# Two-layer block kernel, state-space stage: heads scanned in pairs on opposite column halves, its outputs and the following projection reordered

## The chip, the cores and the metric

The kernel is one program on one core of a Trainium2 chip. Its time is the device time of one launch in microseconds; the figure shown is the median of the launches timed. Engines are named as the profile names them: PE (matmuls), PEld (PE's weight loads), DVE (VectorE), ACT (ScalarE), POOL (GpSimd), SP (the queue that issues the DMAs).

## What is computed

The whole program is a mixer-and-feed-forward block followed by two more such layers, on 512 tokens of width 1024, in float32. The change touches only the second half of the odd layer's mixer: a Mamba-like state-space scan, a gated norm over its 512 channels, and the projection that takes it and four blocks of a multi-scale pool.

```
dt = softplus(dt_raw + dt_bias);  a = -exp(a_log)
y  = ssd_chunked(xh * dt, dt * a, bm, cm)          # 8 heads of 64, 2 groups, state 128
y  = y + d_skip * xh
y  = rms_norm_2(y * silu(z), ssm_norm)             # over all 512 channels of a token
p  = multiscale_pool(pool_in, pool_w, pool_b, pool_scale)
return concatenate([y, p]) @ w_out                 # 1024 x 1024
```

The kernel does the scan in its quadratic form: for a head, y[t] is the sum over s <= t of (cm[t]·bm[s]) · exp(acs[t] − acs[s]) · x[s], with acs the running sum of dt·a.

## The kernel before

Activations stand with channels on the partitions and the 512 tokens on the free axis, so one tile is 128 x 512; `w` is an array of 50 such tiles, and `ps` is the eight banks of PSUM, each 128 x 512 float32. Weights come as a stream of units of eight 128x128 blocks. SP loads a unit into one of three raw buffers (`Weights.load`, L153), ACT rounds it to the high part (`round_high`, L169), POOL subtracts to get the low part (`subtract_low`, L178), and PE takes a product as three matmuls, high·high, high·low and low·high (L321 to L323). Up to three split units exist at once, and a unit's high part waits until the unit three before it has been released by PE. Each stage writes out by hand the order of every engine's instructions; engines meet only in semaphores that count up, and each engine runs its own list in order.

The steps around the change are, in the list at the end of `network`, `odd_in` (the layer's first projection, which leaves silu(z) in the four tiles from ZG, the convolved x in the four from XS, and the pools' outputs in the four from PO), `x_tok` (`to_token_major`, L709 and L720), `ssd`, `odd_out`, and then the feed-forward.

`stage_ssd` (L3032) walks 32 items: two groups, in each four blocks of 128 source tokens (j), in each four heads. For block j only the tokens from 128·j on matter, so its width is 512, 384, 256 or 128 columns. Once per group and block PE forms the query-key product in float32 (L3048) in bank 0 or 1. For each item PE forms the exponent in bank 2 or 3 by three bf16 matmuls (`decay`, L3053 to L3055), ACT takes its exponential into an SBUF tile (L3080), DVE multiplies that with the query-key bank into another (L3089), and PE multiplies x by it (`values`, L3062). That last matmul has 64 columns of weights, and its output goes to the lower or the upper 64 partitions of bank 4 + head//2, by the head's parity. The list of PE is decay(0), then decay(n+1), values(n) for each n, so that two values matmuls always have the three matmuls of a decay between them. A float32 matmul of the program is two matmul instructions in the trace. After the last item DVE adds the skip term (L3095) and applies the gate (L3097), tile by tile.

`odd_out` is `stage_linear` with `before=ssm_norm()`. The norm's part on PE, `factor_pe`, comes first: `column_sums` (L444) over the four tiles of squares, which ACT takes from the gated outputs (L653), then, after a square root on ACT (L464) and a reciprocal on DVE (L470), `spread_columns` (L450). Then `first_products` (L329) makes the first three output tiles at once, input block by input block, in the order 4, 5, 6, 7 (the pools) and 0, 1, 2, 3 (the scan): for each of the first six blocks the high parts of the three (L341, L342) and then the low parts (L347), and the last two blocks output tile by output tile. The high and low parts of all eight blocks are made in this stage by ACT (L649) and DVE (L666), in `odd_split`, tiles 0 to 15; DVE scales the four scan tiles by the factor in bank 7 (L674). ACT begins the stage with the third weight unit that these products need (L2041), POOL with its low part. After the three tiles there is a mean (L2012) and the rest of the product (L321 to L323).

Two other places in the kernel put half-column matmuls next to each other and serve as measures: `narrow_halves` (L391), eight matmuls of 128x64 weights on 512 columns, alternating between the lower and the upper half of bank 4, and the values of the band attention (L1020), for its first pair one matmul of 128 columns on each half.

Of the kernel before, what the change touches and what calls it, by code (L numbers as in the profile page):

```python
# [20 lines left out]
P = 128  # L21
T = 512
# [161 lines left out]
class Before:  # L184
# [3 lines left out]
    def __init__(self, pe, act, dve, pool, high, ready, counts, order=tuple(range(KD))):  # L188
        self.order = order
        self.pe, self.act, self.dve, self.pool, self.counts = pe, act, dve, pool, counts  # L190
        self.high, self.ready = high, ready
# [9 lines left out]
def network(nc, x_t, vectors, constants, rel_rev, stream, bias_line, bias_rows, gate_rows, out_t):  # L201
    n_units = stream.shape[0]
    ctx = ExitStack()
    with ctx:
# [26 lines left out]
        odd_split = split_over("odd_split", 0, KD)  # L231
# [97 lines left out]
        def first_products(pe, rhs, before):  # L329
# [307 lines left out]

        def ssm_norm():

            SQS = 28  # L640
            dst = odd_split

            def pe(p):
                p.wait_ge(norm_act.sem, norm_act.at(4))
                factor_pe(p, [w[:, SQS + t, :] for t in range(4)])

            def act(a):
                def high(t):
                    S.activation(dst[:, 0, t, :], w[:, YS + t, :], ACT.Copy).then_inc(norm_high.sem, 1)  # L649
# [12 lines left out]

            def dve(d):
                def low(t, n):
                    d.wait_ge(norm_high.sem, norm_high.at(n))
                    V.tensor_tensor(dst[:, 1, t, :], w[:, YS + t, :], dst[:, 0, t, :].bitcast(F32),  # L666
                                    ALU.subtract).then_inc(norm_low.sem, 1)

                low(4, 1)
                low(5, 2)  # L670
                factor_dve(d, 5)
                d.wait_ge(norm_pe.sem, norm_pe.at(2))
                for t in range(4):
                    V.scalar_tensor_tensor(w[:, YS + t, :], w[:, YS + t, :], v("ssm_norm", t), bank(FACTOR), ALU.mult,  # L674
                                           ALU.mult).then_inc(norm_dve.sem, 1)
                low(6, 3)
                low(7, 4)
                for t in range(4):
                    low(t, t + 5)

            def place(t):
                return t + 5 if t < 4 else t - 3

            def high_ready(p, t):
                p.wait_ge(norm_high.sem, norm_high.at(place(t)))

            def ready(p, t):
                p.wait_ge(norm_low.sem, norm_low.at(place(t)))

            return Before(pe=pe, act=act, dve=dve, pool=nothing, high=high_ready, ready=ready,  # L690
                          order=(4, 5, 6, 7, 0, 1, 2, 3),
                          counts=((norm_pe, 2), (norm_act, 5), (norm_dve, 5), (norm_high, KD), (norm_low, KD),
                                  (dve_out2, 4)))
# [2195 lines left out]
        XTK, YS, PO = 16, 20, 24  # L2889
# [142 lines left out]
        def stage_ssd():  # L3032


            items = [(g, j, hh) for g in range(2) for j in range(NT) for hh in range(4)]
            n_items = len(items)
            e = [w[:, 46, :], w[:, 47, :]]
            m_ = [w[:, 48, :], w[:, 49, :]]
            @block.tensor
            def _(pe):  # L3040
                def decay(n):
                    g, j, hh = items[n]
                    a, wd = j * P, T - j * P
                    hd = 4 * g + hh
                    if hh == 0:
                        if n >= 8:
                            pe.wait_ge(dve_out.sem, dve_out.at(n - 4))
                        TE.matmul(bank((n // 4) % 2, 0, wd), w[:, BM + g, a:a + P], w[:, CMM + g, a:T],  # L3048
                                  start=True, stop=True)
                    if n >= 2:  # L3050
                        pe.wait_ge(act_out.sem, act_out.at(n - 1))
                    d = bank(2 + n % 2, 0, wd)
                    TE.matmul(d, one_hot(hd, P), row_parts(SSD_PARTS, 0)[:, a:T], start=True, stop=False)  # L3053
                    TE.matmul(d, row_parts(SSD_PARTS, 1)[:, a:a + P], one_hot(hd, wd), start=False, stop=False)
                    TE.matmul(bank(2 + n % 2, 0, P), ident_h[:, :], diag_st_h[:, :], start=False,  # L3055
                              stop=True).then_inc(tile_ready.sem, 1)

                def values(n):
                    g, j, hh = items[n]
                    hd = 4 * g + hh  # L3060
                    pe.wait_ge(dve_out.sem, dve_out.at(n + 1))
                    TE.matmul(bank(4 + hd // 2, j * P, T - j * P, half(hd)), w[:, XTK + j, hd * HD:(hd + 1) * HD],  # L3062
                              m_[n % 2][:, 0:T - j * P], start=(j == 0), stop=(j == NT - 1)
                              ).then_inc(pe_out.sem, 1)
# [3 lines left out]
                for n in range(n_items):  # L3068
                    if n + 1 < n_items:
                        decay(n + 1)  # L3070
                    values(n)

            @block.scalar
            def _(act):
                for n, (g, j, hh) in enumerate(items):
                    wd = T - j * P
                    act.wait_ge(tile_ready.sem, tile_ready.at(n + 1))
                    if n >= 2:
                        act.wait_ge(dve_out.sem, dve_out.at(n - 1))
                    S.activation(e[n % 2][:, 0:wd], bank(2 + n % 2, 0, wd), ACT.Exp).then_inc(act_out.sem, 1)  # L3080

            @block.vector
            def _(dve):
                for n, (g, j, hh) in enumerate(items):
                    wd = T - j * P
                    dve.wait_ge(act_out.sem, act_out.at(n + 1))
                    if n >= 2:
                        dve.wait_ge(pe_out.sem, pe_out.at(n - 1))
                    V.tensor_tensor(m_[n % 2][:, 0:wd], bank((n // 4) % 2, 0, wd), e[n % 2][:, 0:wd],  # L3089
                                    ALU.mult).then_inc(dve_out.sem, 1)  # L3090

                dve.wait_ge(pe_out.sem, pe_out.at(n_items))
                for t in range(4):
                    y = w[:, YS + t, :]
                    dve_chain.link(dve, V.scalar_tensor_tensor(y, w[:, XS + t, :], v("d_skip", t), bank(4 + t),  # L3095
                                                               ALU.mult, ALU.add))
                    V.tensor_tensor(y, y, w[:, ZG + t, :], ALU.mult).then_inc(dve_out2.sem, 1)  # L3097
            tile_ready.close(n_items)
            pe_out.close(n_items)
            act_out.close(n_items)  # L3100
            dve_out.close(n_items)

        def stage_last():
# [44 lines left out]
            ("odd_out", lambda: stage_linear(KD, of(odd_split), "residual", sums="both",  # L3148
# [142 lines left out]
```

## Time and profile before

| | us |
|---|---|
| median of 3 runs (2282.13 to 2284.49) | 2283.25 |
| the profiled execution's own time | 2289.55 |
| its span, first to last instruction | 2287.8 |
| PE busy | 2175.1 (95%) |
| PE weight loads busy | 1754.6 (77%) |
| DVE busy | 996.6 (44%) |
| ACT busy | 839.3 (37%) |
| POOL busy | 818.8 (36%) |

Mean granted TensorE clock of the core: 0.960 of full speed. The chain of work that ended last runs through PE for 86% of the span, through DVE for 8%, ACT for 2% and DMA for 1%. A busy figure is the time in which at least one instruction of an engine was under way; matmuls are pipelined, so PE's is not PE at its peak, and the chain, which counts from one start to the next, is the better measure of what a matmul costs.

### The profile page before, as it was taken

To read this page: it belongs to the slowest core of one execution; us is meant where nothing else is said; L and a number is where in the kernel's file an instruction comes from. 1 tells how busy PE (TensorE), PEld (TensorE's weight loads), DVE (VectorE), ACT (ScalarE), POOL (GpSimd) and SP (SyncE) were. 2 spreads that over 40 slices of the span, in tenths; PEclk is the share of its full clock that TensorE was granted. 3 is DMA by queue.
4 is the path that set the end of the run, shared out by engine and by line. 5 is a ranking of instruction groups with operands and counts; after the bars stand their busy time and mean duration, and the time that the engine had idled before them with its cause. 6 is when DMAs were issued, how large, how long until landed. Compare 5 with 4: busy or idle time off the path is not lost.

```text
span 2287.8 us, 29687 instructions
## 1 busy us (share of the span) xinstructions
PE 2175.1 (95%) x12396; PEld 1754.6 (77%) x12404; DVE 996.6 (44%) x1622; ACT 839.3 (37%) x1284; POOL 818.8 (36%) x362
## 2 busy tenths in 40 slices
PE   7999989999899999999998899999999889999997
PEld 6767778888778888777776678888877477888886
DVE  4222855435631022345337644442268465444323
ACT  4345521133342243243334344442243334444322
POOL 4423300034334444453231344444444035444442
PEclk9999978799999999999999899999999989999998
DMA  7222200014223233222111123323212012332331
GB/s 260 92 74 84 74 2 3 2 56 149 73 83 101 92 102 101 92 65 74 56 56 37 47 92 97 105 93 101 92 64 83 19 56 68 104 96 92 102 100 57
DMA packets 53006, 182.98 MB, mean 80 GB/s; under 512 B 5752, under 2 KB 5760, under 8 KB 52744
## 3 DMA queue, kind: packets, MB, share of 16 engines
q1 hardware_dynamic: 52872, 181.08, 24.6%
q8 instruction: 98, 1.61, 0.3%
q14 instruction: 36, 0.29, 0.0%
HBM read 176.32 MB, written 7.62 MB: 80 GB/s over the span
## 4 chain that ended last, share of the span: by engine, by line
PE 86%; DVE 8%; ACT 2%; DMA 1%; issue 1%; POOL 1%; SPq 0%; DVEq 0%; ACTq 0%
PE ps L321 20%; PE ps L323 20%; PE ps L322 20%; PE ps L1519 3%; PE ps L2526 2%; PE ps L2528 1%; PE ps L2527 1%; PE ps L341 1%; PE ps L347 1%; PE ps L342 1%; PE ps L1049 1%; DMA raw_units<-stream 1%; PE ps L3062 1%; PE ps L1051 1%; PE ps L1050 1%
## 5 line engine op out<-in xcount | busy, mean ns | idle before, releaser
L178 POOL TENSOR_TENSOR split_units<-raw_units,split_units 128x1024 fp32r<-128x1024 f32 x314 | 760.3, 2430 | 1414.5 <-ACT split_units L169 1414.5
L321 PE MATMUL ps<-x_split,split_units 128*128 128x512 f32 x1224 | 483.3, 395 | 10.1 <-POOL split_units L178 7.8
L322 PE MATMUL ps<-x_split,split_units 128*128 128x512 f32 x1224 | 478.7, 391 | 0.0
L323 PE MATMUL ps<-x_split,split_units 128*128 128x512 f32 x1224 | 478.2, 391 | 0.0
L169 ACT ACTIVATE split_units<-raw_units 128x1024 fp32r<-128x1024 f32 x314 | 330.0, 1052 | 387.3 <-PE ps L323 337.9
L321 PEld LDWEIGHTS ps<-x_split,split_units 128*128 128x128 f32 x1224 | 231.1, 189 | 64.5 <-issue 8.0
L322 PEld LDWEIGHTS ps<-x_split,split_units 128*128 128x128 f32 x1224 | 231.1, 189 | 49.4 <-issue 1.7
L323 PEld LDWEIGHTS ps<-x_split,split_units 128*128 128x128 f32 x1224 | 231.2, 189 | 48.7
L321 PE MATMUL ps<-hidden_split,split_units 128*128 128x512 f32 x608 | 237.3, 390 | 0.0
L323 PE MATMUL ps<-hidden_split,split_units 128*128 128x512 f32 x608 | 236.6, 389 | 0.0
L322 PE MATMUL ps<-hidden_split,split_units 128*128 128x512 f32 x608 | 236.5, 389 | 0.0
L2857 DVE SCALAR_TENSOR_TENSOR work<-ps,vec,work 128x511 f32<-128x511 f32 x88 | 66.0, 750 | 225.3 <-ACT work L2846 225.0
L321 PEld LDWEIGHTS ps<-hidden_split,split_units 128*128 128x128 f32 x608 | 114.1, 188 | 24.2 <-issue 0.5
L322 PEld LDWEIGHTS ps<-hidden_split,split_units 128*128 128x128 f32 x608 | 114.1, 188 | 24.1 <-issue 0.5
L323 PEld LDWEIGHTS ps<-hidden_split,split_units 128*128 128x128 f32 x608 | 114.1, 188 | 23.7
L2846 ACT ACTIVATE work<-ps,vec 128x512 f32<-128x512 f32 x88 | 68.7, 781 | 167.9 <-PE ps L323 150.2
L2086 DVE TENSOR_TENSOR x<-x,ps 128x512 f32<-128x512 f32 x29 | 19.9, 688 | 142.4 <-PE ps L323 141.9
L2859 DVE SCALAR_TENSOR_TENSOR work<-ps,vec,work 128x510 f32<-128x510 f32 x88 | 65.9, 749 | 3.1
L2837 ACT ACTIVATE hidden_split<-work 128x512 fp32r<-128x512 f32 x44 | 27.8, 632 | 103.2 <-DVE work L2867 103.2
L1519 PE MATMUL ps<-work 64*64 64x64 f32 x1920 | 62.8, 229 | 0.0
L1519 PEld LDWEIGHTS ps<-work 64*64 64x64 f32 x1920 | 62.5, 146 | 0.0
L341 PE MATMUL ps<-x_split,split_units 128*128 128x512 f32 x120 | 50.8, 423 | 10.6 <-ACT x_split L599 5.0
(436 smaller groups left out, 3274.1 us busy)
## 6 DMA issues: line engine op xcount, KB each, us to landing
raw_units<-stream SPq DMA_DIRECT2D x314, 512.0 KB, 3.5
bias_rows<-bias_line SPq DMA_DIRECT2D x1, 2816.0 KB
gate_rows<-work SPq DMA_DIRECT2D x10, 256.0 KB, 2.1
work<-gate_rows SPq DMA_DIRECT2D x10, 256.0 KB, 2.7
x<-x_t SPq DMA_DIRECT2D x4, 512.0 KB, 6.6
work<-bias_rows SPq DMA_DIRECT2D x1, 2048.0 KB
out_t<-x SPq DMA_DIRECT2D x8, 256.0 KB
vec<-vectors SPq DMA_DIRECT2D x1, 1159.5 KB, 8.6
```

The lines of the kernel that those rows point to most:

```text
L169: scalar.activation(self.split[:, u % SPLIT, 0, :], self.raw[:, u % RING, :], ACT.Copy).then_inc(self.high_done, 1)
L178: gpsimd.tensor_tensor(self.split[:, u % SPLIT, 1, :], self.raw[:, u % RING, :], self.split[:, u % SPLIT, 0, :].bitcast(F32), ALU.subtract ...
L321: TE.matmul(out, high, rhs(0, k), start=(k == 0), stop=False)
L322: TE.matmul(out, high, rhs(1, k), start=False, stop=False)
L323: ins = TE.matmul(out, low, rhs(0, k), start=False, stop=last and shift is None)
L341: TE.matmul(bank(m), high, rhs(0, k), start=(i == 0), stop=False)
L1519: ins = TE.matmul(ps[r, out, i * HD:(i + 1) * HD], left(i, r), right(i, r), start=True, stop=True)
L2526: TE.matmul(bank(b % 2), high, a[0], start=(k == 0), stop=False)
L2837: S.activation(hidden2[:, 0, j, :], w[:, y0 + 2 * j % 4, :], ACT.Copy).then_inc(high_out.sem, 1)
L2846: S.activation(w[:, y0 + m % 4, :], bank(m % 4), ACT.Identity, scale=taps(m)[2], bias=v("ffn_b", layer * 44 + (m % 2) * FF2 + m // 2)).the ...
L2857: dve_chain.link(dve, V.scalar_tensor_tensor(y[:, 1:T], b[:, 0:T - 1], taps(m)[1], y[:, 1:T], ALU.mult, ALU.add))
L2859: V.scalar_tensor_tensor(y[:, 2:T], b[:, 0:T - 2], taps(m)[0], y[:, 2:T], ALU.mult, ALU.add).then_inc(tile_read.sem, 1)
```

## The change

The items become 16 pairs of heads. PE runs two pairs of decays ahead instead of one head, in banks 2 and 3 and, for the odd pairs, 6 and 7; the two values matmuls of a pair stand next to each other, one on each column half. ACT writes its exponentials into tiles 46 to 49 and DVE multiplies in place, so the exponential of pair p waits for the values of pair p − 2. Group 1 reuses banks 4 and 5, so its first values wait for DVE's skip terms of tiles 0 and 1, which now stand behind pair 8; the gates of these two tiles stand behind pairs 9 and 10, their squares (ACT) behind pairs 11 and 12, the sum of these squares (DVE) behind pair 14. The high parts of the pools' blocks are taken by ACT behind pairs 1 to 4, the low parts by POOL. In `odd_out` nothing stands on PE ahead of the products; the column sums come after two input blocks, the spreading after three. The sums are over two tiles instead of four.

```diff
             for i in range(UNIT - APART):
+                if i in before.among:
+                    before.among[i](pe)
                 before.high(pe, before.order[i])
...
-        odd_split = split_over("odd_split", 0, KD)
+        ssm_split, pool_split = split_over("ssm_split", 0, 4), split_over("pool_split", 32, 4)
...
         def ssm_norm():
-            def pe(p):
-                p.wait_ge(norm_act.sem, norm_act.at(4))
-                factor_pe(p, [w[:, SQS + t, :] for t in range(4)])
+            def sums(p):
+                p.wait_ge(norm_dve.sem, norm_dve.at(1))
+                p.wait_ge(norm_act.sem, norm_act.at(4))
+                column_sums(p, SUMS, 4, (w[:, SQS, :], w[:, SQS + 3, :]))
+            def spread(p):
+                p.wait_ge(norm_dve.sem, norm_dve.at(2))
+                spread_columns(p, FACTOR, 8)
             def act(a):
-                for t in range(4):
+                for t in (2, 3):
                     a.wait_ge(dve_out2.sem, dve_out2.at(t + 1))
                     S.activation(w[:, SQS + t, :], w[:, YS + t, :], ACT.Square).then_inc(norm_act.sem, 1)
-                high(4)
-                high(5)
                 factor_act(a, 1, LN_EPS, mean_of=HALF)
-                high(6)
-                high(7)
                 for t in range(4):
-                    a.wait_ge(norm_dve.sem, norm_dve.at(t + 2))
-                    high(t)
+                    a.wait_ge(norm_dve.sem, norm_dve.at(t + 3))
+                    S.activation(ssm_split[:, 0, t, :], w[:, YS + t, :], ACT.Copy).then_inc(norm_high.sem, 1)
             def dve(d):
+                d.wait_ge(norm_act.sem, norm_act.at(3))
+                V.tensor_tensor(w[:, SQS, :], w[:, SQS, :], w[:, SQS + 2, :], ALU.add).then_inc(norm_dve.sem, 1)
                 factor_dve(d, 5)
                 d.wait_ge(norm_pe.sem, norm_pe.at(2))
+                for t in range(5):
+                    if t < 4:
+                        V.scalar_tensor_tensor(w[:, YS + t, :], ...).then_inc(norm_dve.sem, 1)
+                    if t >= 1:
+                        low(t - 1)
+            return Before(pe=nothing, ..., order=(4, 5, 6, 7, 0, 1, 2, 3), among={2: sums, 3: spread}, ...)
...
         def stage_ssd():
-            items = [(g, j, hh) for g in range(2) for j in range(NT) for hh in range(4)]
+            items = [(g, j, pr) for g in range(2) for j in range(NT) for pr in range(2)]
+            FIRST = n_items // 2
+            POOL_AT, GATE_AT, SQUARE_AT, ADD_AT = 1, FIRST + 1, FIRST + 3, FIRST + 6
...
+                def values(p):
+                    g, j, pr = items[p]
+                    pe.wait_ge(dve_out.sem, dve_out.at(2 * p + 2))
+                    if g == 1 and j == 0:
+                        pe.wait_ge(side_dve.sem, side_dve.at(pr + 1))
+                    for hh in range(2):
+                        hd = 4 * g + 2 * pr + hh
+                        ins = TE.matmul(bank(4 + pr, j * P, T - j * P, half(hh)),
+                                        w[:, XTK + j, hd * HD:(hd + 1) * HD], weights(p, hh)[:, 0:T - j * P],
+                                        start=(j == 0), stop=(j == NT - 1))
+                    ins.then_inc(pe_out.sem, 1)
                 decay(0)
-                for n in range(n_items):
-                    if n + 1 < n_items:
-                        decay(n + 1)
-                    values(n)
+                decay(1)
+                for p in range(n_items):
+                    if p + 2 < n_items:
+                        decay(p + 2)
+                    values(p)
+            @block.gpsimd
+            def _(pool):
+                for t in range(4):
+                    pool.wait_ge(norm_high.sem, norm_high.at(t + 1))
+                    G.tensor_tensor(pool_split[:, 1, t, :], w[:, PO + t, :], pool_split[:, 0, t, :].bitcast(F32),
+                                    ALU.subtract).then_inc(norm_low2.sem, 1)
             @block.scalar
+                for p, (g, j, pr) in enumerate(items):
+                    for hh in range(2):
+                        act.wait_ge(tile_ready.sem, tile_ready.at(2 * p + hh + 1))
+                        if p >= 2:
+                            act.wait_ge(pe_out.sem, pe_out.at(p - 1))
+                        S.activation(weights(p, hh)[:, 0:wd], bank(decay_bank(p, hh), 0, wd), ACT.Exp)
+                    t = p - POOL_AT
+                    if 0 <= t < 4:
+                        S.activation(pool_split[:, 0, t, :], w[:, PO + t, :], ACT.Copy).then_inc(norm_high.sem, 1)
+                    t = p - SQUARE_AT
+                    if 0 <= t < 2:
+                        act.wait_ge(dve_out2.sem, dve_out2.at(t + 1))
+                        S.activation(w[:, SQS + t, :], w[:, YS + t, :], ACT.Square).then_inc(norm_act.sem, 1)
             @block.vector
+                    for hh in range(2):
+                        dve.wait_ge(act_out.sem, act_out.at(2 * p + hh + 1))
+                        a = weights(p, hh)[:, 0:wd]
+                        V.tensor_tensor(a, bank((p // 2) % 2, 0, wd), a, ALU.mult).then_inc(dve_out.sem, 1)
+                    if p == FIRST:
+                        dve.wait_ge(pe_out.sem, pe_out.at(FIRST))
+                        skipped(0)
+                        skipped(1)
+                    if 0 <= p - GATE_AT < 2:
+                        gated(p - GATE_AT)
+                    if p == ADD_AT:
+                        dve.wait_ge(norm_act.sem, norm_act.at(2))
+                        dve_chain.link(dve, V.tensor_tensor(w[:, SQS, :], w[:, SQS, :], w[:, SQS + 1, :], ALU.add))
                 dve.wait_ge(pe_out.sem, pe_out.at(n_items))
-                for t in range(4):
-                    dve_chain.link(dve, V.scalar_tensor_tensor(y, ..., bank(4 + t), ALU.mult, ALU.add))
-                    V.tensor_tensor(y, y, w[:, ZG + t, :], ALU.mult).then_inc(dve_out2.sem, 1)
+                skipped(2)
+                skipped(3)
+                gated(2)
+                gated(3)
```

## Rows read from the trace of the kernel before

**Rows 1.** Busy time, granted clock (PEclk) and DMA of stretches of the span.
```profile
core 0: us, PE busy (x) PEld busy (x) DVE busy (x) ACT busy (x) POOL busy (x), PEclk, DMA share, GB/s
1786.80:1829.80 43.00, 41.05 (x174) 15.46 (x176) 15.63 (x32) 14.67 (x33) 0.00 (x0) 1.00 0.00 1
1829.80:1865.10 35.30, 26.77 (x113) 23.43 (x113) 15.71 (x23) 10.94 (x17) 3.63 (x2) 0.76 0.05 15
...
1847.00:1850.60 3.60, 3.60 (x11) 2.87 (x11) 3.14 (x5) 2.29 (x4) 0.00 (x0) 0.51 0.00 0
```
**Rows 2.** Chain that ended last, one head at each width: start, us, what.
```profile
1791.51 1.00 PE ps L3062 x2
...
1796.82 0.79 PE ps L3062 x2
...
1805.25 0.06 PE ps L3054
...
1805.36 0.58 PE ps L3062 x2
...
1807.61 0.36 PE ps L3062 x2
```
**Rows 3.** Timeline of PE: half-column matmuls as neighbours, one alone, and what follows.
```profile
1692.03 3.65 PE L391 MATMUL ps<-x,vec 128*64 128x512 f32 x16
1695.61 0.50 PE L321 MATMUL ps<-x_split,split_units 128*128 128x512 f32 x1
...
1791.29 0.22 PE L3055 MATMUL ps<-diag_st_h,ident_h 128*128 128x128 bf16 x1
1791.44 1.07 PE L3062 MATMUL ps<-work 128*64 128x512 f32 x2
...
98.26 0.44 PE L1020 MATMUL ps<-work 128*64 128x128 f32 x4
98.63 0.50 PE L1049 MATMUL ps<-x_split,split_units 128*128 128x512 f32 x1
```
**Rows 4.** Groups of the scan on ACT and DVE by form, 512 columns wide.
```profile
L3089 DVE TENSOR_TENSOR work<-ps,work 128x512 f32<-128x512 f32 x8 | 5.4, 690 | 9.6 <-ACT work L3080 9.6
L3080 ACT ACTIVATE work<-ps 128x512 f32<-128x512 f32 x8 | 4.7, 596 | 11.6 <-PE ps L3055 11.6
```
**Rows 5.** Timeline around the end of the scan: weight unit, skip term, gate.
```profile
1828.90 1.05 ACT L169 ACTIVATE split_units<-raw_units 128x1024 fp32r<-128x1024 f32 x1
...
1829.86 0.75 DVE L3095 SCALAR_TENSOR_TENSOR work<-work,vec,ps 128x512 f32<-128x512 f32 x1 [0.53 <-PE ps L3062]
1830.03 2.34 POOL L178 TENSOR_TENSOR split_units<-raw_units,split_units 128x1024 fp32r<-128x1024 f32 x1 [49.98 <-ACT split_units L169]
1830.64 2.28 DVE L3097 TENSOR_TENSOR work<-work 128x512 f32<-128x512 f32 x1
```
**Rows 6.** Chain that ended last, from the last gate to the products.
```profile
1836.38 0.70 DVE work L3097
1837.10 0.64 ACT work L653
1837.79 7.00 PE ps L444 x32
...
1845.34 2.08 PE ps L450 x8
1847.42 0.43 PE ps L341
...
1851.44 0.23 PE ps L341
```
**Rows 7.** Timeline: the norm's sums and spreading elsewhere, at full clock and after.
```profile
33.50 1.05 PE L450 MATMUL ps<-con,col 128*128 128x128 f32 x8
...
1895.36 1.95 PE L444 MATMUL ps<-ones,work 128*128 128x1 f32 x16 [0.79 <-DVE work L2095]
...
1899.23 2.08 PE L450 MATMUL ps<-con,col 128*128 128x128 f32 x8 [0.93 <-DVE col L470]
```

More of the change, by code:

```diff
@@ L184, with __init__ @@
 class Before:
-    def __init__(self, pe, act, dve, pool, high, ready, counts, order=tuple(range(KD))):
-        self.order = order
+    def __init__(self, pe, act, dve, pool, high, ready, counts, order=tuple(range(KD)), among=None):
+        self.order, self.among = order, among or {}
         self.pe, self.act, self.dve, self.pool, self.counts = pe, act, dve, pool, counts
@@ L676, in dve @@
[L676 to L682, printed above, removed]
+                for t in range(5):
+                    if t < 4:
+                        V.scalar_tensor_tensor(w[:, YS + t, :], w[:, YS + t, :], v("ssm_norm", t), bank(FACTOR),
+                                               ALU.mult, ALU.mult).then_inc(norm_dve.sem, 1)
+                    if t >= 1:
+                        low(t - 1)
@@ L684, in high_ready @@
             def high_ready(p, t):
-                p.wait_ge(norm_high.sem, norm_high.at(place(t)))
+                p.wait_ge(norm_high.sem, norm_high.at(t + 5 if t < 4 else t - 3))
             def ready(p, t):
[L688 to L693, printed above, removed]
+                if t < 4:
+                    p.wait_ge(norm_low.sem, norm_low.at(t + 1))
+                else:
+                    p.wait_ge(norm_low2.sem, norm_low2.at(t - 3))
@@ L696, in to_token_major @@
+            return Before(pe=nothing, act=act, dve=dve, pool=nothing, high=high_ready, ready=ready,
+                          order=(4, 5, 6, 7, 0, 1, 2, 3), among={2: sums, 3: spread},
+                          counts=((norm_pe, 2), (norm_act, 5), (norm_dve, 6), (norm_high, KD), (norm_low, 4),
+                                  (norm_low2, 4), (dve_out2, 4)))
         def to_token_major(jobs, read, scaled=None):
@@ L3032, in stage_ssd, with weights @@
         def stage_ssd():
[L3035 removed]
+            items = [(g, j, pr) for g in range(2) for j in range(NT) for pr in range(2)]
             n_items = len(items)
[L3037 to L3038 removed]
+            FIRST = n_items // 2
+            POOL_AT, GATE_AT, SQUARE_AT, ADD_AT = 1, FIRST + 1, FIRST + 3, FIRST + 6
+            def weights(p, hh):
+                return w[:, 46 + 2 * (p % 2) + hh, :]
@@ L3039, in _, with decay_bank, decay @@
+            def decay_bank(p, hh):
+                return 2 + 4 * (p % 2) + hh
             @block.tensor
             def _(pe):
-                def decay(n):
-                    g, j, hh = items[n]
+                def decay(p):
+                    g, j, pr = items[p]
                     a, wd = j * P, T - j * P
[L3044 to L3048, printed above, removed]
-                                  start=True, stop=True)
[L3050 to L3064, printed above, removed]
+                    if pr == 0:
+                        if p >= 4:
+                            pe.wait_ge(dve_out.sem, dve_out.at(2 * (p - 2)))
+                        TE.matmul(bank((p // 2) % 2, 0, wd), w[:, BM + g, a:a + P], w[:, CMM + g, a:T],
+                                  start=True, stop=True)
@@ L3093, in _, with skipped @@
[L3093 to L3096, printed above, removed]
-                    V.tensor_tensor(y, y, w[:, ZG + t, :], ALU.mult).then_inc(dve_out2.sem, 1)
-            tile_ready.close(n_items)
+                def skipped(t):
+                    V.scalar_tensor_tensor(w[:, YS + t, :], w[:, XS + t, :], v("d_skip", t), bank(4 + t % 2),
+                                           ALU.mult, ALU.add).then_inc(side_dve.sem, 1)
@@ L3147, in network @@
             ("ssd", stage_ssd),
-            ("odd_out", lambda: stage_linear(KD, of(odd_split), "residual", sums="both",
+            ("odd_out", lambda: stage_linear(KD, odd_half, "residual", sums="both",
                                              before=ssm_norm())),
```

53 lines of the change are left out of this document (28 added, 25 removed).

## The prediction

> **What bounds the kernel now.** I read the table of stretches first, cut where the change begins and ends: from the first query-key matmul of the scan (1786.8) to its last values matmul (1829.8), and from there to the end of the first three output tiles of `odd_out` (1865.1). These are 43.0 and 35.3 us, 78.3 in all, and nothing outside them is touched. In the first stretch the granted clock is 1.00 (2.4 GHz), DVE and ACT are busy for 15.6 and 14.7 us, POOL and the DMAs not at all, and PE for 41.05 of 43.0 us: the scan is bound by PE, and PE idles 1.95 us in it. In the second one the mean clock is 0.76 [rows 1].
>
> Then the chain of waits, to see what PE's time goes to. The values matmul of one head takes 1.00 us of the chain at width 512, 0.79 at 384, 0.58 at 256 and 0.36 at 128 [rows 2]. Each has 64 columns of weights, so it uses half of the array. Eight heads at each width make 8 × 2.73 = 21.8 us, half of the scan. ACT takes 0.60 and DVE 0.69 us for one head at 512 columns [rows 4], less than PE's 1.6 (1.00 and a decay of some 0.6). So two engines have slack and PE has none.
>
> After the scan the chain leaves PE for 8.0 us (1829.8 to 1837.8): DVE's four skip terms and gates, and ACT's last square. The first gate takes 2.28 us, against 0.70 for the last, while POOL's subtraction of a weight unit runs (1830.03 to 1832.37) [rows 5, 6]. PE comes back at half clock: 7.00 us for 32 matmuls of the sums, 0.55 for root and reciprocal, 2.08 for the spreading, and its first products come at 0.43 us each instead of 0.23 [rows 6], 1.2 GHz up to 1850.6 [rows 1]. The products themselves need no sum before their fifth input block.
>
> **The scan, part by part.** *Values in pairs.* What does a pair on opposite halves cost? Where the trace has such neighbours, the two matmuls of 128 columns took 0.37 us to the next start, where one alone takes 0.36; and eight of 512 columns took 3.58 us, 0.45 each, where one alone takes 1.00 [rows 2, 3]. So the second half is nearly free. The bounds are a free second half (0) and none of it free (a full single). I take 0.05 us more than a single: 1.05, 0.84, 0.63, 0.41, four pairs of each, 11.7 us. Saved: 21.8 − 11.7 = 10.1 us.
>
> *Changes between full and half columns.* The third decay matmul starts 0.15 us before a values matmul, though 128 columns of it take 0.06 [rows 2, 3]: 0.09 us for each entry, and 16 fewer of them save 1.4 us. The query-key and decay matmuls stay as they are.
>
> *Waits.* With two pairs of decays ahead, let me see whether ACT and DVE keep up. The exponentials of pair p wait for the values of p − 2. At width 512 two of them and the multiplication behind the second take 2 × 0.60 + 0.69 and some 0.15 of signals, 2.05 us [rows 4]. Meanwhile PE has two decays (1.1), a pair of values (1.05) and two decays again (1.1) to do, 3.25 us. The slack of 1.2 us shrinks with the width to about 0.25 at 128. ACT's four copies for the pools (0.64 each, as a square [rows 6]) stand where the exponentials have to wait for values anyway; only the last, at width 256, delays, by about 0.25 us, and that is inside the slack. POOL's four subtractions of 512 columns, half of 2.34 us each [rows 5], have an idle queue and 43 us. Behind pair 8 DVE waits for the last values of group 0 and adds two skip terms (2 × 0.75): the multiplications of pair 9 are queued behind these, but PE has the query-key matmul of the next block and two decays first; this costs nothing to 0.3 us. The values of pairs 8 and 9 wait for these skip terms, which end sooner than the multiplications. The sum of squares behind pair 14 (0.7) has no cover: the last multiplications are queued behind it and there is no decay left, so it costs its 0.4 to 0.7 us. In all I leave PE 1.25 us of idle time for the 1.95 of before: 0.7 us saved.
>
> The scan: 10.1 + 1.4 + 0.7 = 12.2 us; 43.0 becomes 30.8.
>
> **From the end of the scan.** *Products first.* 72 matmuls at 0.2275 us (the chain's 0.23 at full clock [rows 6]) are 16.4 us. PE can start at once on the first two output tiles, but the third needs the third weight unit. ACT rounds that behind its last exponential and POOL subtracts behind ACT; before, it ended 3.47 us after ACT began [rows 5]. ACT's last exponential will end about 1.1 us ahead of the last values, so the unit is there 2.4 us after the end. PE has 0.9 us of work until then and idles 1.5. This is the late one now, and the norm is not: gate 2 waits for POOL and ends at 3.0 us, gate 3 at 3.7, the last square at 4.3, while PE comes to the sums only at 2.4 + 3.2 = 5.6 us.
>
> *The norm.* 16 matmuls of sums instead of 32, at full clock: 1.95 us, as elsewhere; the spreading 1.05 [rows 7]. Root and reciprocal (0.55) pass beside the third block of products (2.05). Scaling a tile (0.75), its copy (0.64) and its subtraction (0.7) stand beside 2.05 us of products per block and one whole block lies between; if that cover were gone, 2.1 us would show once. ACT's and DVE's work for the pools' blocks is out of this stage.
>
> So 16.4 + 1.5 + 1.95 + 1.05 = 20.9 us for 35.3: 14.4 saved.
>
> **Sum.** 12.2 + 14.4 = 26.6 us. The profiled execution's own 2289.55 becomes 2263.0; it stands 6.3 above the median, of which none is seen in these stretches, so the median 2283.25 becomes 2256.7. What a measurement can tell from no change is about 0.2%, 4.6 us.
>
> **Rivals.** *The pair overlaps only in part (8%).* A float32 matmul is two instructions; if the second head's first had to wait for the first head's second, three streams would follow one another where two suffice: 0.43, 0.32, 0.21 and 0.11 us more per pair, 4.3 in all, and 2261.0. Against it stands the isolated pair of 0.37 us [rows 3]; for it, that no isolated pair of 512 half columns is there. The Trainium skill speaks for this one (TensorE: Matmul & The Clock Gate, Packing small matmuls): matmuls start and end strictly in program order. The isolated pair of 128 columns does not bear it out: by it, that pair would take some 0.46 us, and it took 0.37.
>
> *It does not overlap (5%).* Then the values save nothing, at most 10.1 us back: 2266.8. Against it: eight in 3.58 us.
>
> *The clock falls in the norm (12%).* Sums of one column are light work; at 1895.36 they ran at full rate, but the spreading that followed a little later took 2.08 us instead of 1.05 [rows 7]. In the changed kernel a stretch of PE idling 1.5 us, then sums, stands among the products. If the clock falls there, the spreading costs 1.0 more, the sums up to 1.9, and up to 3.6 us of products at the low level (as from 1847.0 to 1850.6 [rows 1]) 1.8 more: 2258.5 to 2261.5. Against it: dense products stand on both sides.
>
> *Slower (3%).* The clock would have to be down through the scan: it is the only mechanism of the right size. PE's 29.7 us of scan work would double to 59.4, and 3.6 us of products run cold after it (1.8): 2256.7 + 29.7 + 1.8 = 2288.2, slower by 4.9 us. It decides only if nearly all of the scan runs at 1.2 GHz; with half of it the kernel is still faster. Against it: clock 1.00 in the whole of the scan of before, with half of the array idle half of the time and PE waiting more.
>
> *It doesn't do what it says (2%):* another unit or wait, unseen here, holds PE back until the norm is done, and the second stretch stays near its old length: 2271.
>
> **The numbers.** The forecast has 70%, with a range of its own from 2253 (no idle in the scan, a pair at no more than a single, a stall of 0.5) to 2259.5 (waits of 2 us more and a run's scatter of 1). The first three rivals reach 2261.5 and, at the end, 2266.8. The range of 8 in 10 is 2252.5 to 2263.5; it leaves out those that do not overlap and the slower ones. All cases but the slower one are faster by over 4.6 us: with part of its 3% and something for what I have not seen given to no change, that is 0.96 faster, 0.02 within, 0.02 slower.
>
> **What would show it.** In the scan: 31 us between the first L3048-like matmul and the last values, four values instructions of 512 columns in some 1.05 us of the chain, PE idle for 1 to 1.5 us with the largest wait before the last values. After it: no gap of 8 us, the clock at 1.00 through to the third tile, a wait of 1.5 us for POOL's unit, sums of 16 in 1.95 us, spreading in 1.05 us, the products' third tile 21 us after the scan's end. Wrong would be: a pair at 1.5 us or 1.9 (no full overlap), a clock of 0.5 anywhere in it, DVE rather than PE at the end of the waits of pairs 8 to 11, or a wait before the sums.

## The result, and the profile after

The changed kernel took 2258.95 us, the median of 5 runs (2252.35 to 2262.54), against 2284.49 (2282.13 to 2289.44) for the kernel before on the same chip. The ratio on record is 0.9874, with a 95% interval of 0.9855 to 0.9893: faster by 28.8 us, between 24.4 and 33.1. It is not the quotient of these two medians, which lie 25.5 us apart (0.9888). The forecast was 26.6 us less and 2256.7 us. The profiled execution took 2258.95 us (span 2257.2), 30.6 less than the one of before.

First the table of stretches of the changed kernel, with the columns of [rows 1] and cut at the same places: from the first query-key matmul to the end of the last values matmul, and from there to the end of the third output tile. A third one lies further on.

```profile
1786.58:1815.90 29.32, 28.25 (x175) 12.94 (x177) 16.97 (x37) 17.45 (x40) 5.08 (x4) 1.00 0.00 1
1815.90:1836.70 20.80, 19.42 (x97) 16.16 (x97) 10.56 (x16) 7.43 (x11) 3.67 (x2) 1.00 0.09 26
...
1866.70:1916.70 50.00, 46.19 (x203) 38.48 (x204) 24.88 (x41) 25.63 (x37) 26.67 (x15) 0.93 0.20 64
```

The scan went from 43.0 to 29.3 us, the second stretch from 35.3 to 20.8, with the clock at 1.00 where it was 0.76. That is 13.7 + 14.5 = 28.2 us. The other 2.4 us of the 30.6 lie outside of the change, 0.2 ahead of it and 2.2 behind: the norm of the feed-forward, some 30 us later, ran at a mean clock of 0.93 here and at 0.90 in the corresponding 50 us of the kernel before, in code that both have in common.

The chain of waits of the changed kernel, in the scan and from its end on (start, us, what):

```profile
1788.27 1.28 ACT L3104
...
1804.13 0.84 PE ps L3056 x2
...
1805.74 1.01 PE ps L3075 x4
1806.75 0.27 PE ps L3063
...
1807.23 0.16 PE ps L3063
...
1809.80 0.80 PE ps L3075 x4
...
1813.83 0.61 PE ps L3075 x4
1814.69 0.27 ACT work L3104
1814.96 0.95 ACT split_units L169
1815.98 2.38 POOL split_units L178
1818.41 0.50 PE ps L341
...
1821.89 1.68 PE ps L446 x16
...
1825.78 0.89 PE ps L452 x8
```

A pair of values matmuls (L3075, four instructions) now takes 1.01 us at width 512 and 0.80 at 384, where one head alone took 1.00 and 0.79 [rows 2]: the second head costs 0.01. The 8 us on DVE, ACT and an idle PE behind the scan [rows 5, 6] are gone; what the chain names there is the third weight unit, ACT's rounding and POOL's subtraction, for which PE waits. The sums take 1.7 us for 16 instead of 7.0 for 32, the spreading 0.9 instead of 2.1.

The timeline around the end of the scan shows what is late now, and what is not:

```profile
1814.20 0.68 DVE L3139 TENSOR_TENSOR work<-work 128x512 f32<-128x512 f32 x1
1814.52 0.45 ACT L3104 ACTIVATE work<-ps 128x128 f32<-128x128 f32 x2 [0.58 <-PE ps L3075]
1814.85 1.06 ACT L169 ACTIVATE split_units<-raw_units 128x1024 fp32r<-128x1024 f32 x1
1815.47 0.44 PE L3075 MATMUL ps<-work 128*64 128x128 f32 x4 [0.68 <-DVE work L3130]
1815.98 2.37 POOL L178 TENSOR_TENSOR split_units<-raw_units,split_units 128x1024 fp32r<-128x1024 f32 x1 [16.88 <-ACT split_units L169]
1817.28 2.23 DVE L3122 TENSOR_TENSOR work<-work 128x512 f32<-128x512 f32 x2
1818.41 0.50 PE L341 MATMUL ps<-pool_split,split_units 128*128 128x512 f32 x1 [1.38 <-POOL split_units L178]
1818.94 1.23 ACT L659 ACTIVATE work<-work 128x512 f32<-128x512 f32 x2 [3.03 <-DVE work L3122]
1821.73 1.84 PE L446 MATMUL ps<-ones,work 128*128 128x1 f32 x16
```

The two gates (L3122) take 2.23 us, as the first one runs beside POOL's subtraction (with that moved away they take 1.29, further on); the last square ends at 1820.17, 4.3 us after the scan, and PE comes to the sums at 5.8. PE waits 0.68 us before the last pair of values, and 1.38 us for the third unit.

### The profile page after: what moved, and what is told of

The parts are those of the page before. It is cut to its first block, busy times and chain, and to the rows that moved or that the text cites. A ratio compares the mean times of both kernels' runs of the same rounds, so it can differ in the third digit from the quotient of the medians.

```text
span 2257.2 us, 29630 instructions
## 1 busy us (share of the span) xinstructions
PE 2153.4 (95%) x12380; PEld 1743.6 (77%) x12388; DVE 992.0 (44%) x1620; ACT 837.1 (37%) x1284; POOL 823.6 (36%) x366
## 4 chain that ended last, share of the span: by engine, by line
PE 86%; DVE 8%; ACT 2%; DMA 1%; issue 1%; POOL 1%; SPq 0%; DVEq 0%; ACTq 0%
PE ps L321 20%; PE ps L323 20%; PE ps L322 20%; PE ps L1520 3%; PE ps L2527 2%; PE ps L2529 1%; PE ps L2528 1%; PE ps L347 1%; PE ps L341 1%; PE ps L342 1%; PE ps L1050 1%; DMA raw_units<-stream 1%; POOL split_units L178 1%; PE ps L1052 1%; PE ps L1051 1%
```

## The experiments

Whole times scatter by 3 to 12 us over the runs of one kernel on one chip (12 runs of the kernel before: 2281.67 to 2293.23). In the profiled executions the scan's start alone lies anywhere from 1779.3 to 1786.8, in code that all of them share. The two stretches, on the other hand, agree to 0.1 us between two executions of the changed kernel. So the experiments are read from the stretches, and whole times are given beside them. Line numbers of a varied kernel can differ by a few from those of the changed one.

### Both heads of a pair on the same half

```diff
-                        hd = 4 * g + 2 * pr + hh
+                        hd = 4 * g + pr + 2 * hh
-                        ins = TE.matmul(bank(4 + pr, j * P, T - j * P, half(hh)),
+                        ins = TE.matmul(bank(4 + hh, j * P, T - j * P, half(pr)),
```

> The changed kernel with the heads paired as (0, 2) and (1, 3) of a group instead of (0, 1) and (2, 3): the two values matmuls still stand next to each other, but both on the same column half, in two banks. The result is the same computation. Scan = first query-key matmul to the end of the last values matmul (43.0 us before the change, 29.3 after). Theory (the pair is cheap because its two halves of the array run together): a pair then costs about 0.85, 0.64, 0.43 and 0.21 us more at the four widths, four pairs each, 8.5 us more in all, scan about 38 us. Rival (the gain is that two values matmuls stand together, with fewer changes between full and half columns and fewer waits; halves don't matter): scan 29.3 to 30 us. Pair 8 also waits for both skip terms here, at most 0.5 us.

The median was 2263.51 us (ratio to the kernel before 0.9881, 0.986 to 0.9902). The stretches, and the chain in the scan at width 512:

```profile
1779.30:1817.20 37.90, 36.41 (x175) 16.98 (x178) 17.14 (x38) 17.46 (x40) 5.20 (x5) 1.00 0.00 1
1817.20:1837.80 20.60, 19.41 (x97) 16.16 (x98) 10.38 (x16) 7.44 (x10) 3.59 (x2) 1.00 0.10 27
```
```profile
1787.10 1.86 PE ps L3075 x4
```

The scan takes 37.9 us, 8.6 more than in the changed kernel, and a pair 1.86 us instead of 1.01; the surcharge is 0.85, 0.63, 0.43 and 0.22 us at the four widths, one more stream of that width each time. So the two halves of the array do run together, in float32 with different moving data on each. Besides the half, the bank differs: the two heads of a pair now write two banks, where in the changed kernel they share one. No run has opposite halves in two banks, or one half in one bank; that the half decides and not the bank is argued from the size of the surcharge. The rival without overlap is dead as a description of the change, and the one with half an overlap too: it asked for 1.48 us.

### A decay between the two heads

```diff
-                    if p + 2 < n_items:
-                        decay(p + 2)
-                    values(p)
+                    for hh in range(2):
+                        if p + 2 < n_items:
+                            decay(p + 2, (hh,))
+                        values(p, (hh,))
```

> The changed kernel with a decay of one head between the two values matmuls of a pair (decay head 0, values head 0, decay head 1, values head 1), for all pairs but the last two, which have no decays left. Theory: full-column matmuls between them end the overlap, so every values matmul costs its single price again (1.00, 0.79, 0.58, 0.36), and there are 14 more entries at 0.09 us: about 10 + 1.3 us more, scan 40 to 41 us. Rival (order does not matter as the halves are free of each other anyway, or the gain came from looking two pairs ahead): scan about 30 us.

The median was 2272.39 us (0.9927, 0.991 to 0.9944).

```profile
1785.20:1826.40 41.20, 39.53 (x175) 15.22 (x177) 17.16 (x37) 17.42 (x40) 5.05 (x4) 1.00 0.00 1
...
1826.40:1828.90 2.50, 1.13 (x6) 0.61 (x4) 2.44 (x3) 0.04 (x1) 2.37 (x1) 0.89 0.00 0
1828.90:1832.00 3.10, 3.07 (x8) 2.44 (x9) 1.97 (x4) 2.52 (x3) 0.00 (x0) 0.54 0.58 172
```

The scan takes 41.2 us, at the upper end of what was expected, and the chain has the single price again for each head:

```profile
1791.67 1.00 PE ps L3075 x2
```

With full-column matmuls between them, opposite halves give nothing. From the two runs the scan's 13.7 us come apart, roughly. From 43.0 to 41.2 (1.8) more than one thing changes: the last two pairs of this run have no decay left to stand between their heads, so they still overlap (some 0.9 us), PE idles 0.3 us less, and the rest is not told apart; what looking two pairs ahead is worth by itself no run shows. From 41.2 to 37.9 (3.3) it is standing next to each other: two heads on one half take 1.86 us where two apart take 2.00, and one change to full columns falls away for each pair. From 37.9 to 29.3 (8.6) it is the opposite halves.

The second stretch came out at 22.1 us instead of 20.8, which was not asked for. Behind PE's wait of 1.40 us for the third unit the clock is at 0.54 for the next 3.1 us. The changed kernel has the same wait, 1.38 us, and kept its clock in both of its profiled executions.

### The norm first, all else as changed

```diff
+            def first(p):
+                sums(p)
+                spread(p)
-            return Before(pe=nothing, ..., among={2: sums, 3: spread},
+            return Before(pe=first, ...,
```

> The changed kernel with the column sums and the spreading ahead of all products of odd_out, as before the change; all else as changed (sums over two tiles, gates and squares of the first two tiles beside the scan, pools' blocks ready). Second stretch = end of the scan to the end of the third output tile (35.3 us before the change, 20.8 after). Theory A (the order is what saves, and the clock follows PE's idle time): PE idles about 4.4 us until the sum of squares is there, the clock falls to half, sums 3.5 us, 0.55, spreading 2.1, then products 16.4 us with some 1.3 us for their first part at half clock: 28 us. Theory B (a gap of 4.4 us leaves the clock at full): 4.4 + 1.95 + 0.55 + 1.05 + 16.4 = 24.4 us.

The median was 2267.52 us (0.9903, 0.9886 to 0.992). The chain has 3.59 us for the sums and 2.08 for the spreading, and these stretches, the last of them the whole second one:

```profile
1814.70:1819.20 4.50, 0.01 (x2) 0.00 (x0) 4.36 (x6) 1.47 (x4) 2.35 (x1) 0.91 0.22 44
1819.20:1822.80 3.60, 3.57 (x16) 3.49 (x16) 0.00 (x0) 1.05 (x1) 0.00 (x0) 0.50 0.24 93
1822.80:1829.00 6.20, 5.65 (x18) 4.85 (x19) 3.68 (x7) 2.16 (x4) 0.00 (x0) 0.53 0.00 0
...
1814.70:1843.20 28.50, 23.44 (x99) 20.04 (x98) 10.53 (x16) 7.44 (x11) 3.69 (x2) 0.82 0.07 19
```

Theory A: 28.5 us from the scan's end to the third tile. PE idles 4.5 us and then runs at 1.2 GHz for nearly 10 us. Products first save 7.7 us here; 3.1 us of these are the longer idle time (4.5 for 1.4), 0.6 the wait for root and reciprocal, which nothing covers now, and the remaining 4 us are in the main the clock (1.9 in the sums, 1.2 in the spreading).

### The products first, in the kernel before

The scan is left as it was; ACT copies the pools' blocks behind heads 1 to 4, POOL subtracts beside the scan, and `odd_out` has the products first with sums over four tiles.

```diff
+                    t = n - 1
+                    if 0 <= t < 4:
+                        S.activation(pool_split[:, 0, t, :], w[:, PO + t, :], ACT.Copy).then_inc(norm_high.sem, 1)
...
-            return Before(pe=pe, ..., pool=nothing, high=high_ready, ready=ready,
+            return Before(pe=nothing, ..., among={2: sums, 3: spread},
```

> The kernel before with the second part of the change alone: the scan head by head as it was, the pools' high parts on ACT behind heads 1 to 4 and their low parts on POOL during the scan, products first in odd_out, sums (over four tiles, 32 matmuls) after two input blocks, spreading after three. Theory: the scan stays at 43.0 us; in the second stretch PE waits 1.6 us for the third weight unit, reaches the sums 5.7 us after the scan, waits 2.3 us more for gates and squares, sums 3.9 us, spreading 1.05, products 16.4: 25.3 us against 35.3, 10 us faster than before in all. Rival (moving the products changes the second stretch only together with the gates beside the scan): PE waits at the sums much longer and the stretch stays above 30 us. If the clock falls in the wait at the sums, 28 to 29 us.

The median was 2277.49 us (0.9959, 0.9941 to 0.9976), and the scan 43.0 us: the copies and POOL's work cost it nothing. The last row is the whole second stretch.

```profile
1825.10:1829.50 4.40, 2.90 (x12) 2.07 (x13) 4.32 (x5) 0.74 (x2) 2.36 (x1) 1.00 0.20 28
1829.50:1833.00 3.50, 1.68 (x8) 1.05 (x6) 2.92 (x6) 1.88 (x3) 0.00 (x0) 1.00 0.28 115
1833.00:1837.80 4.80, 4.74 (x33) 4.74 (x33) 0.00 (x0) 1.29 (x2) 0.00 (x0) 0.77 0.00 0
1837.80:1842.00 4.20, 4.20 (x12) 3.33 (x12) 0.18 (x1) 0.26 (x1) 0.00 (x0) 0.50 0.02 4
...
1825.10:1853.10 28.00, 24.62 (x112) 20.55 (x113) 13.41 (x19) 8.83 (x13) 3.67 (x2) 0.88 0.07 19
```

The second stretch takes 28.0 us, not the 25.3 of the theory but the branch of the expectation in which the clock falls: PE idles 1.5 us for the unit, 1.9 for the last square, and the clock goes down within the sums. So the order of the products without the shorter norm leaves 28.0 us, and the shorter norm with the first two gates and squares beside the scan, without the order (above), 28.5: 7.3 and 6.8 us for 14.5 together. Both have the pools' blocks ready beside the scan, whose own share no run tells.

### Gates and squares of the first two tiles behind the scan

```diff
-                    if 0 <= p - GATE_AT < 2:
-                        gated(p - GATE_AT)
...
+                gated(0)
+                gated(1)
                 gated(2)
```

> The changed kernel with the gates and squares of the first two tiles back behind the scan; their skip terms stay beside it, since group 1 reuses their banks. Products first, sums over two tiles, as changed. Scan 29.3 us and second stretch 20.8 us in the changed kernel. Theory A (the gates beside the scan are worth little, since PE reaches the sums only 5.6 us after the scan): the last square ends about 5.8 us after the scan's end, the sum of squares 6.5, so PE waits up to 1 us at the sums: second stretch 21 to 22 us, scan 29.2. Theory B (a second wait of PE soon after the one for the third unit takes the clock down, as it did where the products alone were moved): sums, spreading and one to two blocks at half clock, 24 to 26 us.

Their addition moves along with the squares.

```profile
1780.20:1809.40 29.20, 28.23 (x175) 12.91 (x177) 15.34 (x34) 16.35 (x38) 5.07 (x4) 1.00 0.00 1
1809.40:1831.00 21.60, 19.64 (x96) 16.07 (x97) 12.56 (x19) 8.73 (x13) 3.67 (x2) 1.00 0.08 25
```
```profile
1815.94 1.95 PE L446 MATMUL ps<-ones,work 128*128 128x1 f32 x16 [0.48 <-DVE work L674]
```

Theory A: scan 29.2, second stretch 21.6. Gates and squares beside the scan are worth 0.8 us in the second stretch once the products stand first, and cost the scan 0.1. This kernel ran once (2255.45 us). PE waits 1.48 us for the unit and, 3.5 us later, 0.48 at the sums; the clock did not fall.

### The third weight unit during the scan

```diff
                 for p, (g, j, pr) in enumerate(items):
...
+                    if p == 5:
+                        wts.high_part(act, S)
...
-                    wts.round_high(act, S, u0 + 1)
                     before.act(act)
...
+                wts.low_part(pool, G)
```

> The changed kernel with the third weight unit rounded by ACT behind pair 5 and subtracted by POOL behind the pools' blocks, both during the scan, instead of at the start of odd_out. Theory: PE's wait of 1.4 us, 0.9 us into the products, is gone, and the gates of tiles 2 and 3 no longer stand behind POOL (2.2 us for two, should be 1.4): second stretch 19.4 us instead of 20.8, clock 1.00 throughout; scan unchanged at 29.3, or 0.3 us longer where ACT's 1.05 us stands at width 256. Rival (something else is as late as the unit: a buffer or the gates): 20.3 us or more, with a wait at the sums.

The median was 2252.06 us (0.9845, 0.9821 to 0.9869).

```profile
1779.40:1808.70 29.30, 28.21 (x175) 12.90 (x177) 16.95 (x37) 17.36 (x40) 7.43 (x5) 1.00 0.06 19
1808.70:1827.90 19.20, 19.20 (x99) 16.30 (x98) 9.62 (x16) 7.43 (x10) 1.35 (x1) 1.00 0.01 1
```
```profile
1810.11 1.29 DVE L3132 TENSOR_TENSOR work<-work 128x512 f32<-128x512 f32 x2
```

The second stretch takes 19.2 us, with PE busy all the time: it is now nothing but matmuls. The two gates take 1.29 us instead of 2.23, with POOL idle beside them. The scan is as long as in the changed kernel. Its median lies 5.3 us below the changed kernel's on the same chip (2257.34, further on); of these only 1.6 are shown to be the edit's.

### The same, and the exponential's table loaded early

```diff
-                act.wait_ge(tile_read.sem, tile_read.at(0))
                 for p, (g, j, pr) in enumerate(items):
...
+                    if t == 0:
+                        act.wait_ge(tile_read.sem, tile_read.at(0))
```

> As the kernel with the early third unit, and ACT's wait for the stage before moved from ahead of the first exponential to ahead of the first copy. In the changed kernel the table for the exponential was loaded (1.28 us) only when the first exponent was there; before the change it was loaded 5 us earlier. Theory: the load stands ahead of the wait again, the first exponential starts 1.3 us earlier, of which PE gains only the 0.3 us by which it waited for the first pair, since it has two pairs of decays to do: scan 29.0, second stretch 19.4, 1.7 us less than the changed kernel over both. Rival: the scan gains the whole 1.3 us.

```profile
1785.70:1814.60 28.90, 28.09 (x175) 13.11 (x178) 16.97 (x37) 16.09 (x39) 7.44 (x5) 1.00 0.06 19
1814.60:1833.70 19.10, 19.10 (x96) 16.19 (x97) 9.62 (x16) 7.43 (x10) 1.31 (x1) 1.00 0.00 1
```

The scan took 28.9 us and the second stretch 19.1, near the theory's 29.0 and 19.4: of the load's 1.28 us PE feels 0.4. The median was 2258.87 us (0.9873, 0.9851 to 0.9895), 1.5 us above that of the changed kernel on the same chip; the 2.1 us won in the stretches cannot be seen in it.

### The changed kernel again

> The changed kernel once more, unchanged, beside the others: scan 29.3 us, second stretch 20.8 us if the clock stays up behind PE's wait of 1.4 us for the third unit, or 22.1 us if it falls there for the 2.5 us that it fell in the kernel with the values apart. Whole times should again scatter by some 10 us from run to run, by what lies outside of these two stretches.

29.3 and 20.8 us, clock 1.00; the median was 2257.34 us (0.9865, 0.9843 to 0.9887; 2250.94 to 2259.47).

### The sum of squares behind the scan, and a ring of four pairs

Both start from the kernel with unit and table early. The first moves the addition of pair 14 into the norm. The second is

```diff
-                return w[:, 46 + 2 * (p % 2) + hh, :]
+                return w[:, (46, 48, 12, 14)[p % 4] + hh, :]
-                        if p >= 2:
-                            act.wait_ge(pe_out.sem, pe_out.at(p - 1))
+                        if p >= 4:
+                            act.wait_ge(pe_out.sem, pe_out.at(p - 3))
```

> The kernel with the early third unit and the early table (scan 28.8 us, second stretch 19.15), with the sum of the first two squares moved from behind pair 14 to behind the scan. The prediction priced it at 0.4 to 0.7 us of the scan, as the last multiplications are queued behind it. Theory A (the prediction's): scan 28.1 to 28.4. Theory B (what holds the last pair is the exponential, which waits for the values of pair 13, and the sum stands almost wholly beside that): scan 28.7. The sums of the norm start when PE reaches them, 4.1 us after the scan's end, or up to 0.3 us later, as one more sum stands ahead of them on DVE.

> The kernel with the early third unit and the early table, and the exponentials written to a ring of four pairs (tiles 46 to 49 and 12 to 15, which the pools no longer need) instead of two: the exponential of pair p waits for the values of p - 4 instead of p - 2. Theory: the waits of PE before the last pairs (0.7 us before pair 15) shrink, as the exponentials can run ahead as far as the two pairs of decay banks let them; scan 28.1 to 28.4 us instead of 28.8, second stretch 19.15. Rival (PE's own work bounds the scan but for the start, and the last wait is the sum of squares on DVE): scan 28.7 to 28.8.

```profile
1785.80:1814.50 28.70, 28.11 (x177) 13.03 (x177) 16.37 (x36) 16.08 (x39) 7.45 (x5) 1.00 0.06 19
1814.50:1833.90 19.40, 19.40 (x98) 16.19 (x97) 10.31 (x17) 7.43 (x10) 1.31 (x1) 1.00 0.00 1
```
```profile
1785.80:1813.80 28.00, 27.96 (x177) 13.12 (x177) 17.01 (x37) 16.16 (x39) 7.45 (x5) 1.00 0.07 20
1813.80:1833.00 19.20, 19.20 (x99) 16.30 (x98) 9.62 (x16) 7.43 (x10) 1.36 (x1) 1.00 0.00 1
```

Moving the addition (first fence) wins 0.1 to 0.2 us in the scan and loses 0.2 to 0.3 behind it; this kernel ran once (2258.43 us). The ring of four (second fence) wins 0.8 to 0.9 in the scan: PE is busy for 27.96 of 28.0 us. Its two stretches are 47.2 us, against 50.1 in the changed kernel and 78.3 before. Its median was 2259.33 us (0.987, 0.9851 to 0.9889), which cannot be told from the changed kernel's: in the part that the change touches it is 2.9 us better, and the scatter of the whole is larger than that.

## Why the prediction was right, and where its terms were off

The time forecast was 2256.7, measured 2258.95, inside of the range; the gain forecast was 26.6 us and the interval is 24.4 to 33.1. By the stretches it was 28.2: the scan gave 1.5 us more than forecast and the second stretch 0.1 more. With a scatter of some 10 us between single executions, that the whole time came within 2.3 us of the forecast is in part luck; the stretches are the test.

*What bounds the scan.* PE, as read. That PE keeps the pace in pairs too, is shown by the busy times: 28.25 of 29.32 us.

*Values in pairs:* 11.7 us forecast, 4 × (1.01 + 0.80 + 0.58 + 0.37) = 11.0 measured. The lower bound, a free second half, was nearly right; that it comes from the halves is what the pair on one half speaks for.

*Changes between full and half columns.* 1.4 us forecast, at 0.09 for each entry to half columns. The chain shows the price on the way back: the first decay matmul takes 0.27 us at width 384 behind values, 0.16 behind another decay, 0.11 less once for each pair, which makes an estimated 1.8.

*Waits.* 1.25 us of idle PE forecast, 1.07 measured, with the largest wait before the last values, as forecast, but not for the reason given. The sum of squares, priced at 0.4 to 0.7, is worth 0.1 to 0.2: the step "there is no decay left, so it costs" overlooked that the exponential of pair 15 is held by the values of pair 13 (the 0.58 us wait for L3075 at 1814.52), and the addition (1814.20 to 1814.88) stands beside that. The ring of four shows it: the wait is gone, for 0.8 us. And the table load was not in the forecast: it came back onto the path with a wait put ahead of the first exponential, at 0.4 us. The 0.28 us that PE waited before the first pair and the 0.68 before the last make up nearly all of its idle time. 12.2 us were forecast for the scan and 13.7 came; values (0.7), changes (0.4) and idle time (0.2) account for 1.3 of the 1.5 missing, and the other 0.2 stay open.

*Behind the scan:* 20.9 forecast, 20.8 measured, with small errors that cancel. The wait for the third unit was 1.4 for 1.5, the last square 4.3 us after the scan for 4.3, the sums reached at 5.8 for 5.6, and the sums and the spreading took 1.7 and 0.9 us of the chain for 1.95 and 1.05. The forecast had added their whole durations (1.84 in the timeline here), where the chain counts from start to start; the products took by difference 16.9 us for 16.4. That the unit is the late thing is shown by its being moved: 1.6 us, with the gates no longer beside POOL.

*The rivals.* Half an overlap and none: fell with 1.01 us for a pair of 512 columns. The rule of the Trainium skill behind the first (TensorE: Matmul & The Clock Gate, Packing small matmuls), that matmuls start and end in program order, did not bring what the rival read from it: four instructions in 1.01 us leave no room for three streams in a row, which would take 1.48. In what order the four ended, the merged rows do not show. The fall of the clock did not come in the two executions of the changed kernel that were profiled, but it came in its variants: behind the wait for the unit with the values apart (1.3 us), behind the 4.5 us of idle time with the norm first, and with the products alone moved, where a wait of 1.5 us was followed by one of 1.9. It did not come with the gates last, where the second wait was 0.5 us. So the price was of the right kind, but it falls behind waits of PE, not with the one-column sums as such: these ran at full clock in the changed kernel. The slower case had no sign of itself: 1.00 through every scan. (Its sum has 29.7 us for PE's work in the scan; 41.05 − 10.1 − 1.4 is 29.55, which changes nothing.)

What stays open is why the clock held behind a wait of 1.2 to 1.5 us for the unit in three kernels and fell in one, and what makes the whole time scatter ahead of the scan.

## What to carry to other kernels

Two half-column matmuls on opposite halves cost one only where they stand next to each other; a full-column matmul between them, or the same half, takes the overlap back (scans of 41.2 and 37.9 us against 29.3). The wait for a norm's sums can be covered with products of another input, and the larger part of the profit may be the clock that a shorter gap keeps up (4 of 7.7 us here). When a wait is gone, ask for the next late thing on every queue: here it was a weight unit that stood behind the last exponential on ACT, and after that the two-deep ring.

## What the runs showed of the hardware

- Opposite column halves overlap in full in float32, with different weights and moving data: 1.01 us for two matmuls of 512 columns, 1.86 on the same half (and in two banks). Put apart by full-column matmuls they took 1.00 each.
- PE's granted clock fell to half (1.2 GHz) after an idle time of 4.5 us, after 1.5 and 1.9 us with 3.5 us between them, and once after a single 1.40 us; after 1.38 us (the changed kernel, twice), 1.19 (same half) and 1.48 (gates last) it stayed up.
- Two DVE multiplications of 128x512 with both inputs in SBUF took 2.23 us while a POOL subtraction ran beside the first, and 1.29 us without it. The two skip terms, which read one input from PSUM, took 1.41 us either way.
- The exponential's table load (1.28 us), which the program does not write out, moved with the waits ahead of the first exponential: with one wait the load ran 5 us before its data (1783.11 and 1788.47 in the kernel before), with a second one it ran only when these had come (1788.27 and 1789.57 in the changed one).
- Over 12 runs of the kernel before on one chip the time spread by 11.6 us, while the two stretches of the changed kernel were the same to 0.1 us in its two profiled executions. Changes of 2 us in a kernel of 2260 are seen in stretches alone.
